# Modulation rows on TensorE in place of identity products at the edges of a two-layer block, and the last FFN step's operands in a place of their own

## The reference

```python
c_act = jax.nn.silu(c)
for l in range(2):
    ada = c_act @ w_ada[l] + b_ada[l]
    sh1, sc1, gt1, sh2, sc2, gt2 = jnp.split(ada, 6)
    u = x * (1.0 + sc1) + sh1
    y = mixer(u, ...)
    x = layer_norm(ALPHA * x + (1.0 + gt1) * y, ln_mix_g[l], ln_mix_b[l])
    u = x * (1.0 + sc2) + sh2
    h = jnp.square(jax.nn.relu(u @ w_up[l])) @ w_down[l]
    x = layer_norm(ALPHA * x + (1.0 + gt2) * h, ln_ffn_g[l], ln_ffn_b[l])
```

## Time and profile before

| what | us |
|---|---|
| median of 3 runs | 1808.67 |
| lowest and highest run | 1807.61, 1810.6 |
| the profiled execution | 1806.2 |
| its span | 1804.6 |
| PE busy | 1747.3 (97% of the span) |
| DVE busy | 1275.0 (71%) |
| ACT busy | 891.1 (49%) |
| share of the 16 DMA engines, SP's queue | 58.8% |

### The profile page before, as it was taken

The page is one execution under the profiler, slowest core; times in us unless marked ns, Lnnn a source line. Parts: engine busy times, 40 slices in busy tenths (PEclk is TensorE's granted clock), DMA queues, the critical chain, the costliest instruction groups (busy, mean ns, idle before and its releaser), DMA issues.

```text
span 1804.6 us, 26736 instructions
## 1 busy us (share of the span) xinstructions
PE 1747.3 (97%) x9254; PEld 1445.8 (80%) x9254; DVE 1275.0 (71%) x1973; ACT 891.1 (49%) x1530; POOL 54.8 (3%) x111
## 2 busy tenths in 40 slices
PE   8999999998999999998999999999999999999998
PEld 3775778996766779987998977788789989778886
DVE  5688897667788885568557987555555588865555
ACT  2456334443455444444656664444455667544443
POOL 0000010000000000001000000000000000000000
PEclk9999999999999999999999999999999999999999
DMA  8866568774766666663764434656556635355563
GB/s 313 265 220 215 166 222 300 253 230 141 253 215 205 192 214 207 208 189 104 238 215 155 141 117 152 185 183 190 173 175 187 212 123 161 127 154 180 181 190 124
DMA packets 216040, 346.29 MB, mean 192 GB/s; under 512 B 19611, under 2 KB 113353, under 8 KB 215673
## 3 DMA queue, kind: packets, MB, share of 16 engines
q1 hardware_dynamic: 213448, 338.89, 58.8%
q0 software_dynamic: 1632, 5.39, 1.0%
q10 hardware_dynamic: 850, 0.54, 0.1%
HBM read 343.69 MB, written 1.07 MB: 191 GB/s over the span
## 4 chain that ended last, share of the span: by engine, by line
issue 79%; PE 14%; DVE 4%; DVEq 1%; POOLq 1%; POOL 1%; ACT 0%; ACTq 0%
PE acc L150 2%; PE acc L148 2%; PE acc L149 2%; PE prod L223 2%; PE prod L225 1%; PE prod L224 1%; DVE w_lo L134 1%; PE prod L148 1%; DVE proj L938 1%; DVEq L937 1%; PE prod L149 1%; PE prod L150 1%; PE turn L262 1%; DVE stats L927 0%; DVE x_res L1223 0%
## 5 line engine op out<-in xcount | busy, mean ns | idle before, releaser
L134 DVE TENSOR_TENSOR w_lo<-w_raw,w_hi 128x1024 fp32r<-128x1024 f32 (+2 forms) x584 | 643.5, 1122 | 308.1 <-ACT w_hi L128 302.3
L128 ACT CAST w_hi<-w_raw 128x1024 fp32r<-128x1024 f32 (+2 forms) x584 | 557.9, 968 | 408.2 <-PE acc L150 185.5
L148 PE MATMUL prod<-w_hi,hT_hi 128*128 128x512 f32 (+2 forms) x880 | 318.7, 362 | 2.2 <-ACT proj_b L1979 1.1
L150 PE MATMUL prod<-w_hi,hT_lo 128*128 128x512 f32 (+2 forms) x880 | 312.0, 355 | 0.0
L149 PE MATMUL prod<-w_lo,hT_hi 128*128 128x512 f32 (+2 forms) x880 | 311.3, 354 | 0.0
L148 PEld LDWEIGHTS prod<-w_hi,hT_hi 128*128 128x128 f32 x880 | 165.4, 188 | 22.8 <-DVE gates L2232 5.9
L150 PEld LDWEIGHTS prod<-w_hi,hT_lo 128*128 128x128 f32 x880 | 165.4, 188 | 15.4
L149 PEld LDWEIGHTS prod<-w_lo,hT_hi 128*128 128x128 f32 x880 | 165.8, 188 | 14.6
L223 PE MATMUL prod<-uT_hi,w_hi 128*128 128x256 f32 x448 | 127.0, 284 | 0.6 <-ACT proj L882 0.6
L148 PE MATMUL prod<-w_hi,uT_hi 128*128 128x512 f32 x304 | 124.6, 410 | 2.7 <-DVE uT_lo L301 1.3
L224 PE MATMUL prod<-uT_lo,w_hi 128*128 128x256 f32 x448 | 126.4, 282 | 0.0
(11 more groups left out here) (349 smaller groups left out, 2823.6 us busy)
## 6 DMA issues: line engine op xcount, KB each, us to landing
w_raw<-in_w_in_dram SPq DMA_DIRECT2D x72, 512.0 KB, 3.9
ada_raw<-in_w_ada_dram SPq DMA_DIRECT2D x68, 512.0 KB, 6.8
w_raw<-in_w_in_dram SPq DMA_DIRECT2D x192, 172.0 KB, 2.6
w_raw<-in_w_up_dram SPq DMA_DIRECT2D x64, 512.0 KB, 4.5
w_raw<-in_w_down_dram SPq DMA_DIRECT2D x64, 512.0 KB, 4.6
w_raw<-in_w_gate_dram SPq DMA_DIRECT2D x128, 192.0 KB, 2.5
w_raw<-in_w_ffn_gate_dram SPq DMA_DIRECT2D x88, 256.0 KB, 3.6
w_raw<-in_w_ffn_up_dram SPq DMA_DIRECT2D x88, 256.0 KB, 4.3
```

Of the source, the lines that this page charges most:

```text
L128: act.copy(self.hi[:, s, 0:cols], self.raw[:, s, 0:cols]).then_inc(self.hi_done, 1)
L134: dve.tensor_tensor(self.lo[:, s, 0:cols], self.raw[:, s, 0:cols], self.hi[:, s, 0:cols].bitcast(F32), ALU.subtract).then_inc(self.lo_done, 1)
L148: pe.matmul(out, a_hi, w_hi, start=first and c == 0, stop=False)
L150: mm = pe.matmul(out, a_lo, w_hi, start=False, stop=last and c == chunks - 1)
```

## The change

`gt2` is made as two more halves (m = 6 and 7). Their `mod_rows` stand at the middle edge, ahead of the first turn and behind it, where the identity products were, and their two `mod_sum` follow the turned tile. In layer 1 halves 0 and 1 move from behind tiles 1 and 3 to the two places around the first turn of the layer. `gate2_chunk`, its loads and the sum ahead of the last `down` are gone. The loads of half 6 go behind the second group of `w_out`, those of half 7 behind the last; those of layer 1's half 1 behind `down(2)` of layer 0's FFN, of half 0 ahead of its last `down`. Three of these halves ("placed") lie in free columns of `proj` and not in `ada_raw`. Both sums of the next layer's rows stand together in the middle of `down(6)`, the second in the banks of the turns. The last step's squares go to `lastT`, in `uT`, right behind the relu. And DVE makes the next scale and shift ahead of the low part of the last weight group.

```diff
-    def turned_tile(..., awake, before, after, halved):
-        awake(0, before)
+    def turned_tile(..., ahead, behind, halved):
+        ahead()
         turn(0)
-        awake(1, after)
+        behind()
@@ buffers
+        lastT = tuple(part[:, 0:4, :] for part in uT)
-        ada_acc = proj[:, 0, 0:D]
-        gate2_raw = [proj[:, slot, GC0:GC0 + D] for slot in range(2)]
+        half_places = [[proj[:, tok, at:at + D] for at in (second, GC0) for tok in range(TOKS)] for second in (GA0, D)]
+        MIXES, HALVES = 2 + PAIRS, 4 + PAIRS
+        PLACED = [(0, HALVES - 1), (1, 1), (1, HALVES - 1)]
@@ SP, w_out and FFN
+                        if at == G_IN + 2 * G_HALF + 2:
+                            half_bias(HALVES - 2)
+                            half_rows(HALVES - 2)
+                        if at == G_IN + 2 * G_HALF + 8:
+                            half_bias(HALVES - 1)
+                            sp.wait_ge(merged, layer(l, 3, 4).count(1))
+                            half_rows(HALVES - 1)
-                sp.wait_ge(merged, layer(l, 3, 4).count(1))
-                gate2_rows(0)
                 for f in range(T_FF - 1):
                     if l < LAYERS - 1:
                         next_first(f + 1)
                     up(f + 1, Pos(at + 4, (l, G1), (f, 8)))
-                    gate2_rows(f + 1)
                     down(f, Pos(at + 8, (l, G1), (f, 8)))
+                    if l < LAYERS - 1 and f == 2:
+                        W.wait_used(sp, layer(l, at + 3, G1))
+                        half_bias(1, l + 1)
+                        half_rows(1, l + 1)
+                if l < LAYERS - 1:
+                    half_bias(0, l + 1)
+                    half_rows(0, l + 1)
                 down(T_FF - 1, layer(l, at + 4 + 8 * (T_FF - 1), G1))
@@ ACT, first tile of layer 1; middle edge; FFN
                     for n in range(4):
+                        if n == 0:
+                            part_take(0, prod[0])
                         take_u_hi(n)
+                        if n == 1:
+                            part_take(1, prod[1])
...
+                    if n < 2:
+                        part_take(HALVES - 2 + n, acc[n])
...
+                    if f == T_FF - 1:
+                        squares(f, tile, lastT)
                     split(before + 3, 1)
                     if sums:
                         split(before + 4, 1)
                         sums(1)
-                        split(before + 5, 2)
                         sums(0)
-                        split(before + 7, 1)
+                        split(before + 5, 3)
@@ DVE, hidden(), last step
                     if f == T_FF - 1:
-                        gate2_chunk(f)
-                    if after:
+                        hidden_lows(f, lastT)
+                        split(after + (-1), 1)
+                        split(after, 3)
+                        following_rows()
+                        split(after + 3, 1)
+                    elif after:
                         split(after)
@@ PE
+                def vacated_first(tok):
+                    if l > 0:
+                        pe.wait_ge(part_taken, layer(l, tok, HALVES).count(1))
+                    vacated(layer(l, 0, N_TILES))(tok)
+                def ahead_first():
+                    if l > 0:
+                        pe.wait_ge(ada_taken, layer(l - 1, SUMS - 1, SUMS).count(3))
+                        mod_rows(0, prod[0])
+                def behind_first():
+                    if l > 0:
+                        mod_rows(1, prod[1])
+                    else:
+                        T.awake(pe, layer(l, F_U + 1, F_ALL), 3)
...
-                              lambda n, k: T.awake(pe, layer(l, F_U2 + n, F_ALL), k), 4, 3,
+                              lambda: mod_rows(HALVES - 2, acc[0]), lambda: mod_rows(HALVES - 1, acc[1]),
                               lambda n: T.halved(pe, layer(l, S_U2 + n, S_ALL)))
+                for n in range(2):
+                    mod_sum(HALVES - 2 + n, acc[n])
...
-                pe.wait_ge(gate2_used, layer(l, T_FF - 1, T_FF).count(3))
-                if l < LAYERS - 1:
-                    pe.wait_ge(ada_taken, layer(l, HALVES + 1, SUMS).count(3))
-                sum_rows(prod, ada_acc, True)
```

More of the change, by code:

```diff
@@ L189, in multiply, with turned_tile @@
                 between()
-    def turned_tile(self, pe, pos, lhs, width, outs, turn, taken, vacant, awake, before, after, halved):
-        awake(0, before)
+    def turned_tile(self, pe, pos, lhs, width, outs, turn, taken, vacant, ahead, behind, halved):
+        ahead()
         turn(0)
-        awake(1, after)
+        behind()
         for tok, out in enumerate(outs):
@@ L793, in scalar @@
                 split(layer(l, 11, G1), 1)
-                part_take(0)
+                if l == 0:
+                    part_take(0)
                 hpad_take(0, l)
@@ L871, in scalar, with squares @@
                               view=lambda s: s.rearrange("p (c t) -> p c t", c=4))
+                    if n < 2:
+                        part_take(HALVES - 2 + n, acc[n])
                 at += 4
+                def squares(f, tile, place):
+                    for b in range(2):
+                        act.wait_ge(prod_free[b], tile.count(2))
+                        act.activation(place[0][:, 2 * b:2 * b + 2, :].rearrange("p c t -> p (c t)"), r_rows[:, b, :], ACT.Square)\
+                           .then_inc(hidden_hi, 1)
                 def hidden(f, tile, last_group, fill, before, after, sums=None):
@@ L1419, in u_turn, with mod_rows @@
                     rows_turn(layer(l, F_U + n, F_ALL), u_rows[:, n // 2, :], 4 * (n % 2))
+                def mod_rows(m, bank=acc[0]):
+                    if placed(l, m):
+                        pe.wait_ge(place_in, 64 * (order_of(l, m) + 1))
+                    for i in range(4):
+                        if placed(l, m):
+                            raw = half_place(l, m)[i]
+                        else:
+                            pe.wait_ge(ada_in[i], layer(l, 4 * raw_half(l, m) + i, FILLS).over(4).count(1, 16))
+                            raw = ada_raw[:, i, :]
+                        for k in range(2 * i, 2 * i + 2):
+                            c = k % 4 * 32
+                            mm = pe.matmul(bank[c:c + 32, :], c_wide[:, k, 0:32], raw[:, k % 2 * NT:(k % 2 + 1) * NT],
+                                           start=k < 4, stop=k >= 4)
+                        if not placed(l, m):
+                            mm.then_inc(ada_used[i % 2], 1)
+                    if placed(l, m):
+                        mm.then_inc(place_used, 1)
```

206 lines of the change are left out of this document (103 added, 103 removed).

## The result

The changed kernel takes 1798.53 us (median of four: 1796.82, 1797.22, 1799.83, 1800.94) beside 1808.59 for the kernel before: ratio 0.9946, 95% interval 0.9933 to 0.996. Run again later beside another set of the kernel before it took 1800.02 (median of five, 1796.32 to 1800.45), ratio 0.9951 (0.9937 to 0.9964). The median of all nine runs is 1799.83. The forecast was 1799.9, with a change of -8.8; the medians of the two sets differ from their kernels before by -10.1 and -8.3.

What follows compares the result with a forecast made beforehand. The prediction took PE, busy 97% of the span, to bound the kernel. Its terms -4.5 - 3.9 + 2.6 - 3.0 summed to -8.8 us, a median of 1799.9 us, with a range from 1797.5 to 1803.8.

Steps and rivals of the forecast that it cites:

- Layer 0's end: End of layer 0: fewer sums and waits and an earlier scale and shift bring PE and DVE forward, -4.5 us.
- A stall of some 0.2, on the edge: Layer 0's last `down`: PE waits some 0.2 us for the last low part of the weights.
- First tile: Layer 1's first tile: modulation rows replace identity products, their extra time hidden by PE's 1.34 us wait; 0 us.
- `w_in`: Layer 1's `w_in` tiles, where PE is full: two halves of modulation rows leave, -3.9 us.
- DVE eats half: Rival in layer 1's tiles: DVE takes half the gain, total -6.9, 1801.8 us; chance 0.20 together with the moved wait.
- Middle edges: Middle edges of both layers: two new `mod_sum` behind the tile, 1.28 us each after 0.44 hidden; +2.6 us.
- Layer 1's end: End of layer 1: the `gt2` sum and the low-part waits go, second half's residual at 816.8; -3.0 us.
- Free items: `gate2_chunk` leaving DVE, the first sum's second place, and moved loads, four of them ahead of weights: taken as 0 us.
- no cast at 206 or 273 us waits longer: Sign to look for: casts at 206 and 273 us wait no longer for a transfer than before.
- late weights: Rival: half 6's loads delay `w_out`'s third group by 3 us, each middle edge 1.5 later; total -5.8, chance 0.13.
- The clock: Rival at three edges: without identity products PE's clock halves, +27.6 us, net +18.8, 1827.5 us; chance 0.04.
- 11.2 more, 2 of it in idle time: Step of the clock rival: a turned tile's 48 products at half speed cost 9 us at each of three edges.

Runs made afterwards that it cites:

- the operands' place alone: Kernel before with only the last FFN step's squares and low parts put in a part of uT, right behind the relu; 1805.95 us, ratio 0.9984.
- the half that was put back by itself: Changed kernel with layer 1's half 0 back behind the second `w_in` tile, four identity products ahead of the first turn; 1799.11 us, ratio 0.9949.
- the sums inside: Changed kernel with `mod_sum` pairs inside the turned tiles, at both middle edges and layer 1's first tile; 1793.69 us, run again 1795.26.

## Why the prediction was right

**Layer 0's end, -4.5.** Measured -3.85 from the sums of `down(6)` on, so 0.65 too high. Of this 0.4 is a slip in the sum: the moved pair was taken at 1.32, and by the prediction's own reckoning a pair costs 1.72, the longer first product behind it included. The last `down` starts 4.12 earlier for that, not 4.5. DVE inherits the slip: its third low part of the last weights waits for a cast, and that cast for PE to be through with the slot. This low part,

```profile
418.51 1.23 DVE L134 TENSOR_TENSOR w_lo<-w_raw,w_hi 128x1024 fp32r<-128x1024 f32 x1 [0.67 <-ACT w_hi L128]
```

ended 0.66 later than reckoned (415.16, which is 419.74 less the distance of 4.58, and not 414.5), 0.4 by the slip and the rest on its own, and the first residual starts 3.85 earlier and not 4.5. "A stall of some 0.2, on the edge" was 0.30. The mechanism stands: without the moved scale and shift 1.76 is lost, the operands' place alone gives 1.19, and the turn moved by what DVE's first residual did, 3.85, not by PE's 4.12.

**First tile, 0.** By the distances 0: +0.74 at the first turn, +1.51 at the second quarter, +0.74 again at the third. The cover was named rightly: 1.34 became 0.56.

**`w_in`, -3.9.** Measured -3.89 and -3.72, and the half that was put back by itself lost its 1.96. The rival "DVE eats half" did not come: DVE is busier (26.95 us in the window where it had 24.87), and PE waits for it in one new place, by 0.25 us (457.85).

**Middle edges, +2.6.** Measured +2.31. The term took the two sums at 1.72 with 0.44 covered; 1.15 each is what they cost. I missed that the same cover that made the rows free had 1.2 us left, in two waits, for the sums: the experiment that moved them took the term to 0.04.

**Layer 1's end, -3.0.** Measured -3.29, with the last `down` at its predecessor's end (808.79). The second half's residual stands here:

```profile
814.61 0.69 DVE L1263 SCALAR_TENSOR_TENSOR proj<-ada_rest,acc 128x512 f32<-128x512 f32 x1
```

That is 816.56 with the distance of -1.95 taken off, where 816.8 was forecast, and it no longer waits for PE.

**Free items.** The loads ahead of weights: no wait of PE came from them in either profile of the changed kernel. But "no cast at 206 or 273 us waits longer" was wrong at both places. The cast of `w_out`'s third group, before and after:

```profile
206.41 1.05 ACT L128 CAST w_hi<-w_raw 128x1024 fp32r<-128x1024 f32 x1
```

```profile
211.74 1.05 ACT L128 CAST w_hi<-w_raw 128x1024 fp32r<-128x1024 f32 x1 [1.49 <-DMA w_raw<-in_w_out_dram]
```

With the distance of 3.72 taken off it is 1.6 later, and it waited 1.83 us in the second profile. All eleven profiles with the added loads have this wait, from 1.06 to 2.13 us; the three without them have none. So the mechanism of the rival "late weights" did come, with 1.6 to 1.9 us of delay where it named 3, and cost nothing: the distance at the turns of `w_out` and at the middle edge stays at +3.72. The slack that the rival put at 1.5 is thus larger than it said. In `up(1)` the cast at 279.42 waited 1.64 us for its transfer, where its like before waited 0.29; PE wanted it later still. The slack is thin there: the kernel with the operands' place alone has no load added and still lost 1.38 us at that very place.

**The clock.** I gave this rival 9 us an edge. It did not come, as the clock stayed up with what replaced the identity products, but my reason was half wrong: the clock does hang on them, and it is the price that is small, because DVE bounds the edge. The rival's step that failed is "11.2 more, 2 of it in idle time".

**The sum** of the terms is -8.8; the timelines give -9.0 and -8.8. This is closer than the terms were: layer 0's end was 0.65 too high, and the 0.30 at `up(1)`, which stands in no term, with 0.3 each from the middle edges and layer 1's end, made up for it. That the median of nine runs came within 0.1 us of the forecast is luck too: single runs of this kernel lie 4.6 us apart, and the first four had 1798.53.

## What to carry to other kernels

Where another engine sets an edge, look for every wait that is left in it and fill each with work that is needed anyway; rows were moved here and the sums were not, which left 3.5 us. For changes below 0.2%, compare the starts of the same instruction stage by stage: a median can hide 1.95 us that a timeline shows to 0.1. And start such a step at a row right ahead of the stage, or a wait that lies between is put down to it (0.3 to 1.4 us at `up(1)` here). A gap filled with idle work helps only if nothing behind it waits as well.

## What the runs showed of the hardware

- The start has two speeds. The same products took 592 ns or up to 1222, until 11 to 13 us in six profiles, until 17 in two and until 23 in two (with the changed code and with the sums inside); with 13 products of `ones` ahead they ran at full speed from the first on, in four of four profiles. In the first profile of the changed kernel the clock's column says 1.00 from 8 to 16 us while products of twice the time run; in the second, with half speed only until 11.5, it says 0.60 at 9 to 12. So the column alone does not clear a stretch: the products' own durations must be read.
- Half speed at 1.2 GHz is not the same as time lost: some 7 us of it at layer 1's first tile cost 0.6, and 3.5 us at layer 0's middle edge nothing, as DVE bounds both.
- Behind waits of 0.47, 1.20 and 0.94 us the clock fell in 7 of 24 last pairs, and behind the same waits in the others it did not.
